# Squared tiles of a norm group added on GpSimd before a single product with ones, and the expert bias splits moved behind the last addition

## What is computed

```python
def group_rms(y, g):
    return (y * lax.rsqrt(jnp.mean(jnp.square(y), axis=-1, keepdims=True) + RMS_EPS)) * g

y = concat([group_rms(y_lru, g_lru),      # 512 channels
            group_rms(y_swa, g_swa),      # 256 channels
            group_rms(y_sb,  g_sb)])      # 256 channels
mixed = y @ w_out + b_out
h = layer_norm(DN_ALPHA * h + mixed, ln1_g, ln1_b)
ff = moe_ffn(h, w_router, b_router, w_exp_in, b_exp_in, w_exp_out, b_exp_out)
```

## Time and profile before

| | |
|---|---|
| median of 3 runs | 1474.34 us (1472.99 to 1474.62) |
| the profiled execution's own time | 1474.43 us |
| its span, first to last instruction | 1472.7 us |
| granted TensorE clock, mean | 0.991 of full speed |
| PE (TensorE) busy | 1427.1 us, 97% |
| DVE (VectorE) busy | 1214.7 us, 82% |
| ACT (ScalarE) busy | 975.7 us, 66% |
| POOL (GpSimd) busy | 490.6 us, 33% |
| HBM traffic | 319 GB/s over the span |

### The profile page before, as it was taken

How to read it: one execution, slowest core, us unless ns; L and a number is a source line. 1 busy time by engine, 2 the same in 40 slices (tenths; PEclk the granted TensorE clock), 3 DMA queues, 4 the chain that set the end, 5 groups by cost and what they waited for, 6 DMA issues and landing times.

```text
span 1472.7 us, 20375 instructions
## 1 busy us (share of the span) xinstructions
PE 1427.1 (97%) x6495; PEld 1095.9 (74%) x6495; DVE 1214.7 (82%) x1002; ACT 975.7 (66%) x710; POOL 490.6 (33%) x309
## 2 busy tenths in 40 slices
PE   6999989998999999999999999999999999999995
PEld 3466554776888888888888888888888888888873
DVE  5533357577999999999999999999999999999985
ACT  2244660176777777777777777777777777777762
POOL 4200125152333334344333444443343333333101
PEclk9999999999999999999999999999999999999997
DMA  7221226479999999999999999999999999999933
GB/s 260 76 61 36 61 104 261 186 270 360 367 378 379 377 386 385 380 377 371 376 378 384 379 380 390 385 387 382 381 380 378 379 378 381 379 379 378 359 122 126
DMA packets 86310, 461.43 MB, mean 313 GB/s; under 512 B 11912, under 2 KB 26506, under 8 KB 37130
## 3 DMA queue, kind: packets, MB, share of 16 engines
q1 hardware_dynamic: 75190, 431.91, 74.6%
q0 software_dynamic: 9648, 26.49, 7.8%
q10 hardware_dynamic: 1444, 2.66, 0.7%
HBM read 443.92 MB, written 25.76 MB: 319 GB/s over the span
## 4 chain that ended last, share of the span: by engine, by line
PE 75%; DVE 1%; DMA 1%; POOL 1%; issue 1%; POOLq 0%; DVEq 0%; ACT 0%; ACTq 0%
PE banks L1765 69%; PE banks L1733 2%; PE banks L1739 2%; DMA acc_dram<-glu_lin 1%; PE banks L1797 1%; POOL sel L1464 1%; PE banks L1860 0%; POOLq L1466 0%; DVE raw L1694 0%; PE banks L1865 0%; DVEq L1585 0%; DVE raw L1698 0%; PE banks L1727 0%; DVE glu_lin L1581 0%; ACT hi L1352 0%
## 5 line engine op out<-in xcount | busy, mean ns | idle before, releaser
L1544 DVE TENSOR_TENSOR lo<-raw,hi 128x2048 fp32r<-128x2048 f32 x384 | 867.1, 2289 | 75.8 <-ACT hi L1352 75.5
L1352 ACT ACTIVATE hi<-raw 128x2048 fp32r<-128x2048 f32 x384 | 733.7, 1920 | 249.6 <-PE banks L1765 249.4
L1765 PE MATMUL banks<-hi,x_hi 128*128 128x512 f32 x1040 | 286.7, 397 | 8.8 <-DVE x_lo L1568 6.5
L1765 PE MATMUL banks<-lo,x_hi 128*128 128x512 f32 x1040 | 280.1, 391 | 0.0
L1765 PE MATMUL banks<-hi,x_lo 128*128 128x512 f32 x1040 | 278.9, 389 | 0.0
L1464 POOL TENSOR_SCALAR sel<-cst,rank_e 128x128 bf16<-128x128 f32 x120 | 209.7, 1759 | 136.9 <-issue 136.9
L1765 PEld LDWEIGHTS banks<-lo,x_hi 128*128 128x128 f32 x1040 | 195.9, 188 | 41.9
L1765 PEld LDWEIGHTS banks<-hi,x_lo 128*128 128x128 f32 x1040 | 195.4, 188 | 41.4
L1765 PEld LDWEIGHTS banks<-hi,x_hi 128*128 128x128 f32 x1040 | 190.7, 188 | 47.3 <-issue 11.2
L1487 POOL DMA_INDIRECT acc_dram<-ye,dst_row x31 | 50.2, 1620 | 363.5 <-ACT ye L1377 363.5
L1765 PE MATMUL banks<-hi,a_hi 128*128 128x512 f32 x496 | 155.7, 395 | 0.0
(11 more groups left out here) (276 smaller groups left out, 1198.5 us busy)
## 6 DMA issues: line engine op xcount, KB each, us to landing
raw<-in_w_exp_in SPq DMA_DIRECT2D x256, 1024.0 KB, 7.7
raw<-in_w_exp_out SPq DMA_DIRECT2D x128, 1024.0 KB, 7.2
raw<-in_w_in SPq DMA_DIRECT2D x9, 1024.0 KB, 7.6
raw<-in_w_out SPq DMA_DIRECT2D x4, 1024.0 KB, 5.1
x<-in_x SPq DMA_DIRECT2D x4, 512.0 KB, 6.2
h_dram<-x SPq DMA_DIRECT2D x4, 512.0 KB, 3.2
bias_in<-bias_dram SPq DMA_DIRECT2D x128, 3.0 KB
raw<-acc_dram SPq DMA_DIRECT2D x4, 512.0 KB, 5.3
```

The source lines that it names most:

```text
L1352: act.activation(hi[:, c0 % PARTS, :], raw[:, c0 % RAW, :], ACT.Copy).then_inc(hi_done, 1)
L1544: dve.tensor_tensor(lo[:, c0 % PARTS, :], raw[:, c0 % RAW, :], hi[:, c0 % PARTS, :].bitcast(F32), ALU.subtract).then_inc(lo_done, 1)
L1765: last = pe.matmul(psum[:, bank + n, :], s[:, k, :], w[:, at:at + 512], start=(first and m == 0 and new), stop=(closes and m == steps - 1 ...
```

## The change

GpSimd gets a new function, `add_squares(g)`. It waits until a group's squares are there and adds them pairwise in place: three additions of 128x512 for group 0 (two, a drain, one), one each for groups 1 and 2. It then adds one to a new semaphore, `sq_added`. TensorE's job q waits for that one and makes a single product with ones in place of one per tile. On GpSimd the additions of group 0 come ahead of the masking of head 3, those of groups 1 and 2 behind it, and both `split_biases` come behind those.

```diff
+                def add_squares(g):
+
+                    tiles = GROUPS[g][1]
+                    step = len(tiles) // 2
+                    pool.wait_ge(y_sq, normed_by(g))
+                    while step:
+                        for c in range(step):
+                            to = squares[tiles[c]]
+                            last = pool.tensor_tensor(to, to, squares[tiles[c + step]], ALU.add)
+                        step //= 2
+                        if step:
+                            pool.drain()
+                    last.then_inc(sq_added, 1)
+
                 for h in range(4):
+                    if h == 3:
+                        add_squares(NORM_ORDER[0])
                     pool.wait_ge(w_exp, h + 1)
...
                     last.then_inc(w_ready, 1)
-                    if h >= 2:
-                        split_biases(h - 2)
+                for g in NORM_ORDER[1:]:
+                    add_squares(g)
+                for h in range(2):
+                    split_biases(h)
                 pool.drain()
...
                         g = int(name[1])
-                        tiles = GROUPS[g][1]
-                        pe.wait_ge(y_sq, normed_by(g))
-                        for c in tiles:
-                            last = pe.matmul(bank, ones, squares[c], start=(c == tiles[0]), stop=(c == tiles[-1]))
-                        last.then_inc(job_ready, 1)
+                        pe.wait_ge(sq_added, NORM_ORDER.index(g) + 1)
+                        pe.matmul(bank, ones, squares[GROUPS[g][1][0]], start=True, stop=True).then_inc(job_ready, 1)
                         return
```

More of the change, by code:

```diff
@@ L355, in hybrid_layer @@
         lru_exp, lru_om, lru_sqrt, lru_out = sem("lru_exp"), sem("lru_om"), sem("lru_sqrt"), sem("lru_out")
-        y_sq, yn_ready = sem("y_sq"), sem("yn_ready")
+        y_sq, sq_added, yn_ready = sem("y_sq"), sem("sq_added"), sem("yn_ready")
         out_ready, out_added = sem("out_ready"), sem("out_added")
```

## The result

The changed kernel takes 1491.8 us (median of 4 runs, 1490.71 to 1492.24), the kernel before 1474.48 us in the same comparison. The ratio is 1.0115, 95% interval 1.0101 to 1.0129: 17 us slower. The profiled execution took 1491.78 us and its span is 1490.0 us, 17.3 us more than before.

What follows compares the result with a forecast made beforehand. TensorE, busy 97% of the span, was taken as the bound; transposes 10.3 us later (0.9 us of longer q jobs inside) plus 1.7 us of lower clock made 12.0 us: 1486.4 us, range 1479.5 to 1491.

Steps and rivals of the forecast that it cites:

- Additions in place of products: Group 0's squares before job q0: GpSimd's three additions take 3.6 us with drain and hand-over, and the root is not late.
- The other branch: At q0, additions and VectorE's two subtractions from PSUM block each other: softmax chain and sum some 1.2 us larger.
- q1 and q2: TensorE's jobs for groups 1 and 2: addition with hand-overs 1.25 us against 0.9 saved; projection starts 0.9 us later.
- The first split, moved: GpSimd's first bias split starts at 216.9 us, takes 15.6 us under contention and ends at 232.5 (228.2 to 234.7).
- I take 244: Landing of the late LayerNorm loads beside SyncE's six loads: 244 us, between bounds of 239.9 and 246.7.
- I take 1.5: VectorE's first LayerNorm tile meets the second split on GpSimd: 1.5 us of waits added to its 7.3 us.
- I add it once: Lower granted clock behind TensorE's 9 us gap before the transposes: 1.7 us, with nothing or twice this possible.
- The rest is moved and covered: Bias store, h1 stores and GpSimd's scaling of tile 0 come later, hidden by TensorE's two projections of 14 us.
- loads in time: LayerNorm loads land by 235.6 us, leaving only 0.9 us of longer q jobs: 1475.3 us, no change; chance 0.04.
- a little faster: Additions with hand-overs cost less than the products replaced and loads come in time: at best 1473.2 us; chance 0.02.
- the fourth (milder): LayerNorm loads land at 239.9 us, little contention, no clock loss: 4.7 us later, 1479 us; chance 0.10.
- The third: More blocking: additions block VectorE's subtractions, landing 247, three waits on the tile, clock loss 3.4 us: 1494 us; chance 0.07.

Runs made afterwards that it cites:

- e2: Changed kernel with the first bias split put back between the maskings of heads 2 and 3, additions kept: 1476.95 us, ratio 1.0017.
- e9: Changed kernel with 50 unused products filling TensorE's gap before the transposes of h1's first tile: 1486.75 us, ratio 1.0081.
- e1: Changed kernel with ScalarE's two LayerNorm loads issued ahead of its wait for the first split: 1475.99 us, ratio 1.0009.
- e8: Kernel before with additions for group 0 alone, two products each for groups 1 and 2, splits unmoved: 1475.00 us, ratio 0.9997.
- e4: Changed kernel with SyncE's six 1 MB loads held until the LayerNorm gain and bias have landed: 1481.17 us, ratio 1.0049.
- e7: Changed kernel with the LayerNorm loads ahead of the bias loads, both still behind the wait for the first split: 1486.92 us, ratio 1.0080.

## Why the prediction was right in its mechanism and wrong in its size

The place, the chain and the sign were as predicted. The time, 1491.8 us, lies above the range's end of 1491.0. By its own steps:

- **"Additions in place of products", q0: right.** The three additions took 3.55 us (3.6 predicted) and the root was not late. VectorE's two subtractions from PSUM beside them took 0.69 and 0.95 us and did not wait. That is what the Trainium skill (SBUF — State Buffer, "Who interferes with whom") states for one SBUF input outside the two-port modes, and this trace agrees, where the trace before could not show it. The other branch, 1.2 us more, did not come.
- **q1 and q2: too small.** "The rest of the projection starts 0.9 us later": it was 3.5, of which 0.4 stood there ahead of q0. The additions and products took little more than predicted (1.32 us, 1.1 us, and hand-overs of 0.23 instead of 0.1), but behind the 3.58 us of gap before q1 the granted clock was 0.67: q1 took 1.43 us and the values of head 3 3.73 instead of 2.32, together 1.7 us. The prediction put the clock at nothing there, without a reason. In e2 and e9 the window values lost the same 1.6 us instead. This miss is not added to the landing below but acts through it: y was done 3.3 us later than before, and with it SyncE's six loads began later.
- **"The first split, moved": right at its end, by two errors that cancel.** It began at 219.36 instead of 216.9 and took 12.7 us instead of 15.6. The prediction let it meet four scalings of y and two or three L836; it met two of those scalings, since the other two were over, and a reciprocal of 3.35 us (from 221.42), beside which GpSimd's subtraction and cast took 2.12 and 1.03 us, as in their quiet time. End: 232.0 against 232.5, by luck.
- **"I take 244": this step failed.** The landing was at 249.75, behind even the upper bound of 246.7. The prediction stood between equal shares of the bytes (242) and "after every byte of both queues" (246 to 246.7), and the second was what happened: from 234 us to the landing ScalarE's queue got 1.44 of 5.79 MB, 25%, near the 23% of the earlier trace rows, and SyncE's queue was all but empty at the end. That is 2.7 of the missed 5.7 us. The other 3.0 are the start of the bound: the six loads began to move at 228.9 and not at 226, since y was done later. The bound's rate was good by luck: the traffic took 20.85 us at 364 GB/s, against 20.7 at 373, although it was 282 in one stretch of six us and 421 in the next. The Trainium skill's rule (DMA: Bandwidth & Descriptors, "Queues, rings and completion order"), turns by the packet, was read as equal bytes. The profile's packets, one row of a load each, were indeed equal in number, 167 to 161, but not in size; whether they are the packets of that rule no run shows. This is the largest miss: 5.7 us.
- **"I take 1.5" for contention in the first tile: too high.** It was 0.1 us: by 253.6, when VectorE came to L872 (L854 before), GpSimd was at its last cast. With 5.7 - 1.4, and a hand-over of 0.05 us where 0.2 was counted, the transposes were 14.45 us later instead of 10.3.
- **"I add it once": the clock term was 1.7, measured 3.0** (e9; "twice this" was named as possible). The lower level lasted longer behind 10.8 us of gap than behind the 2.2 us from which it was taken.
- **"The rest is moved and covered": right.** GpSimd's scaling, the h1 stores and the bias store, at 254 instead of 236, delayed nothing. From the expert block's first transposes (299.58 before, 316.06 after, +16.5) to the end another 0.8 us came, within what executions differ by. The +17.4 us behind the projection of tile 2 became +16.5, because a stretch of idle products ahead of the routing, at a clock of 0.64 in the trace before (4.79 us), ran in 3.17 us, of which half a us was lost again behind it. This is no gain of the change: of the eleven traces five have the shorter stretch, e1 and e8 among them.

Sum, as measured: 14.45 + 2.97 - 0.94 + 0.8 = 17.3 us, against 10.3 + 1.7. Of the rivals, the first two (loads in time, a little faster) are excluded by the rows of VectorE; the fourth (milder) needs the landing in 5.6 us and no clock loss, which only e4 had. The third was nearest in size (1494) with its late landing (247) and its 3.4 us of clock, but its 5.7 us of blocking did not come.

## What to carry to other kernels

Before work is moved on one engine, look at who waits for its end and what is queued behind that waiter: here two 0.5 MB loads that nobody had moved stood behind a wait for the moved work, and became the bound. A load that is issued late also meets other traffic; price its landing with the packets of both queues, not with its landing when alone, and put the load that someone will wait for ahead of the one that is not urgent (e7, by order alone, brings the landing forward by 4.1 us; e1, ahead of the wait as well, gives back all but about 1 us of 17). Replacing products by additions on a slower engine gains nothing where the product is shorter than the addition plus two hand-overs, 0.9 against about 1.5 us here, and a gap on TensorE costs more than its length, here 10.8 us and 3.0 more.

## What the hardware showed that was not expected

- Two DMA queues in company got equal numbers of packets (167 to 161 in 6 us; a packet of the profile is one row), so the one with 4 KB packets got about a third of the bytes beside the one with 8 KB.
- While the bias loads went, the sum of both fell to 282 GB/s from 421, with the DMA engines as busy as before; the dip moved with these loads in e7. The cause is open.
- TensorE's clock was 0.50 for all of the 5.8 us looked at behind a gap of 10.8 us, and 1.00 behind one of 3.07 us (e4). Behind gaps of 2.8 us before q0 and 3.6 before q1 it was lower behind one and full behind the other, and not the same one in every execution; the loss was 1.6 to 1.7 us in all seven traces that have both. So a gap of 2.8 us can cost more than one of 3.07, and the length of a gap alone does not tell.
